# First pair of the up-projection as plain products, with new orders at three stage changes, in a one-core decoder trunk

## The chip, the cores and the metric

One Trainium2 chip, one of its cores. The metric is the device time of one execution of the whole program, in microseconds (us); the kernel before has a median of 1436.61 us over 3 runs (1431.98 to 1438.98).

## The reference, cut to what matters

```python
def reference(x, norm_mix, w_in, ..., w_out, norm_ffn, w_up, conv_w, conv_b, w_down):
    h = rms_norm(x, norm_mix[i])
    proj = h @ w_in[i]
    ...                      # three token mixers: NSA, S5, stick-breaking
    merged = (merge_g[:, :, 0] * (o_a @ w_br_nsa[i])
              + merge_g[:, :, 1] * (o_b @ w_br_s5[i])
              + merge_g[:, :, 2] * (o_c @ w_br_sb[i]))
    x = x + merged @ w_out[i]
    x = x + conv_ffn(rms_norm(x, norm_ffn[i]), w_up[i], conv_w[i], conv_b[i], w_down[i])

def conv_ffn(h, w_up, conv_w, conv_b, w_down):
    u = h @ w_up
    u = causal depthwise convolution of width 3 over the tokens, + conv_b
    gate, val = jnp.split(u, 2, axis=-1)
    return (jax.nn.gelu(gate) * val) @ w_down
```

x is 1024 tokens by 1024 features, float32; w_up is 1024 by 4096, w_down 2048 by 1024.

## The kernel before, in words

Every float32 product is made of three fp32r products (`mm3`, L910 to L914): each operand is split into a high part (an ACT or POOL copy that rounds to fp32r) and a low part (the operand minus its high part), and high by high, high by low and low by high are summed in PSUM. So one 128x128 by 128x512 block costs three MATMUL instructions on PE.

**The token-mixing part** ends with 8 merge panels for the NSA branch (P_NSAMERGE + k, k from 0 to 7, called M+k here) and 8 output panels (P_OUT + k, k from 0 to 7). SP loads each panel into one of two `raw` slots, POOL splits it (`split_panel`, L772 and L775), PE multiplies it. Each merge panel is 60 MATMULs, each output panel 48.

**The sums of down-projection weights.** The up- and the down-projection use a Strassen-Winograd scheme: 7 half-size products in place of 8, on sums of blocks of the weights and of the activations. For the down-projection the four weight sums V are made ahead, beside the last merge panels, in 8 rounds e: SP loads four 128x512 blocks into `vsum` (`load_v`, L599), POOL adds them in place (`sum_v`, L845, four instructions), SP stores them to DRAM (`save_v`, L605). There is one `vsum` buffer, in `arena2`: the load of round e+1 waits for the store of round e. POOL does the sum of round e right after it has split panel M+1+e, so POOL's order is split, sum, split, sum, 8 times, the last after the split of P_OUT.

**The second norm.** When the residual x2 is complete, ACT and DVE normalise it in 8 tiles of 128 tokens (`norm_tiles`, L1540, L1891), PE transposes them (`norm_transposes`, L929) in two halves of tokens T0 and T1, 8 groups of 128 features each. Half T0 is split straight out of PSUM into hTh and hTl (ACT L1551, DVE L1899). Half T1 is handled by the code after that: in this order the kernel before makes the low sums s3, s4, s2 and so on that the Winograd scheme wants (ACT L1828 to L1841, DVE L2418 to L2436, POOL L888, L895, L900), for the four kinds of left operand "n2", "s1", "s4", "s3" of `UP_LEFT`, kept in `hxh`/`hxl` (12 blocks each) and in hTh/hTl.

**The up-projection** has 16 column pairs j (128 gate columns and 128 value columns). A pair is 7 pieces i = 0 to 6 of 12 MATMULs each (`up_product`). `STREAM` lists all pieces in the order of PE; every weight piece n of it is made high by ACT (`weight_high`, L1764) and low by POOL (`weight_low`, L868), with the pair's weight sums on POOL (`weight_sum`, L863) in between. Slots: 5 for raw weights, 5 for the split ones; piece n on ACT waits until PE has used piece n-5. Between pieces ACT copies PSUM banks (`copy_x`, `copy_z`) and DVE adds them (`up_add`, L2445); piece 3 of a pair waits for the copy after piece 1, piece 4 for the one after piece 2. After piece 6, ACT starts the convolution (`conv_first`, L1773) and DVE adds the two other taps (L2453, L2455), ACT applies the GELU and DVE multiplies (L2464, `ffn_pair`).

```python
        STREAM = [(0, 0), (0, 1), (1, 0), (0, 2), (0, 3), (0, 4), (1, 1), (0, 5), (1, 2), (0, 6), (1, 3), (1, 4)]
        for j in range(2, 16):
            STREAM += [(j, 0), (j - 1, 5), (j, 1), (j - 1, 6), (j, 2), (j, 3), (j, 4)]
```

**The down-projection** has 56 pieces ("dn", c) of 12 MATMULs, 7 products m of 8 pieces. Activations are split in 28 halves-pairs f, high by ACT (`dn_high`, L1815), low by DVE (`dn_low`, L2492), with sums of activation blocks before (`dn_sum`, L2478 to L2484) and in place after (L2497, L2502). Product m is added to the output by DVE (`y_out`, L2515), and product m+2 or so, which reuses its PSUM banks, waits for it (`DN_AFTER`). Six of the activation blocks had been spilled to DRAM and are read back (`act_back`, L725).

## Time and profile before

| what | value |
|---|---|
| median of 3 runs | 1436.61 us |
| the profiled execution, its own time | 1430.5 us |
| its span, first to last instruction | 1428.8 us |
| mean granted TensorE clock | 0.978 of 2.4 GHz |
| PE / DVE / POOL / ACT busy | 93% / 55% / 44% / 36% |

The span is cut in 40 slices of 35.7 us in the profile's second part; PE is at 9 tenths or more in most of them, with clear dips in the first slice and around slice 27 (929 to 964 us). The stages at the end are: NSA merge panels from 708 us, output panels from 819 us, the norm from 914 us, the up-projection from 918 us (in steady repetition from 987 us), the down-projection from 1260 us.

### The profile page before, as it was taken

To read this page: it belongs to the slowest core of one execution; us is meant where nothing else is said; L and a number is where in the kernel's file an instruction comes from. 1 tells how busy PE (TensorE), PEld (TensorE's weight loads), DVE (VectorE), ACT (ScalarE), POOL (GpSimd) and SP (SyncE) were. 2 spreads that over 40 slices of the span, in tenths; PEclk is the share of its full clock that TensorE was granted. 3 is DMA by queue.
4 is the path that set the end of the run, shared out by engine and by line. 5 is a ranking of instruction groups with operands and counts; after the bars stand their busy time and mean duration, and the time that the engine had idled before them with its cause. 6 is when DMAs were issued, how large, how long until landed. Compare 5 with 4: busy or idle time off the path is not lost.

```text
span 1428.8 us, 18621 instructions
## 1 busy us (share of the span) xinstructions
PE 1332.2 (93%) x7133; PEld 1052.1 (74%) x7133; DVE 784.8 (55%) x1281; ACT 510.4 (36%) x971; POOL 627.8 (44%) x418
## 2 busy tenths in 40 slices
PE   5999889999999899999899989859999999999998
PEld 4888456799777666666688868637888888877886
DVE  5797576534554766666535211563444444469932
ACT  5422554400111244444311100444454554454431
POOL 4212003234723111101267653578777777756642
PEclk9999999999999999999999999969999999999999
DMA  7430101042111000000145451302222111155433
GB/s 188 47 54 19 45 1 31 16 79 56 38 31 44 19 19 19 1 19 19 49 155 182 166 218 52 133 15 70 79 89 74 55 57 54 53 169 184 131 96 140
DMA packets 142007, 106.01 MB, mean 74 GB/s; under 512 B 41680, under 2 KB 115792, under 8 KB 141904
## 3 DMA queue, kind: packets, MB, share of 16 engines
q1 hardware_dynamic: 141920, 104.83, 25.0%
q8 instruction: 57, 0.93, 0.3%
q14 instruction: 30, 0.25, 0.1%
HBM read 84.76 MB, written 20.05 MB: 73 GB/s over the span
## 4 chain that ended last, share of the span: by engine, by line
PE 74%; DVE 9%; POOL 5%; DMA 4%; ACT 4%; issue 3%; SPq 1%; ACTq 0%; DVEq 0%; POOLq 0%
PE ps L912 20%; PE ps L913 19%; PE ps L914 19%; PE ps L1394 3%; POOL arena L845 3%; PE ps L1427 2%; DMA arena<-in_w_down 2%; PE ps L1411 2%; PE ps L1152 1%; DMA v_down<-arena 1%; PE ps L1169 1%; PE ps L1182 1%; DVE arena L1891 1%; PE ps L929 1%; DVE merged L2139 1%
## 5 line engine op out<-in xcount | busy, mean ns | idle before, releaser
L868 POOL TENSOR_TENSOR wl<-raw,wh 128x512 fp32r<-128x512 f32 x168 | 236.4, 1411 | 158.9 <-ACT wh L1764 158.9
L912 PE MATMUL ps<-hTh,wh 128*128 128x512 f32 x752 | 302.8, 403 | 2.7 <-ACT arena L1630 1.9
L914 PE MATMUL ps<-hTh,wl 128*128 128x512 f32 x752 | 294.1, 391 | 0.0
L913 PE MATMUL ps<-hTl,wh 128*128 128x512 f32 x752 | 294.1, 391 | 0.0
L772 POOL TENSOR_TENSOR wh<-raw,zero 128x1280 fp32r<-128x1280 f32 (+2 forms) x37 | 82.1, 2220 | 478.5 <-PE ps L914 463.1
L1764 ACT ACTIVATE wh<-raw 128x512 fp32r<-128x512 f32 x168 | 105.8, 632 | 305.4 <-PE ps L914 248.8
L912 PE MATMUL ps<-wh,hTh 128*128 128x512 f32 (+2 forms) x496 | 174.0, 351 | 6.7 <-DVE conv L2515 3.4
L914 PE MATMUL ps<-wh,hTl 128*128 128x512 f32 (+2 forms) x496 | 173.9, 351 | 0.0
L913 PE MATMUL ps<-wl,hTh 128*128 128x512 f32 (+2 forms) x496 | 173.6, 350 | 0.0
L775 POOL TENSOR_TENSOR wl<-raw,wh 128x1280 fp32r<-128x1280 f32 (+2 forms) x45 | 128.9, 2865 | 94.6 <-ACT wh L1576 91.7
L912 PEld LDWEIGHTS ps<-hTh,wh 128*128 128x128 f32 x752 | 141.7, 188 | 37.4 <-issue 7.2
L914 PEld LDWEIGHTS ps<-hTh,wl 128*128 128x128 f32 x752 | 141.6, 188 | 31.0
L913 PEld LDWEIGHTS ps<-hTl,wh 128*128 128x128 f32 x752 | 141.7, 188 | 27.6 <-issue 0.5
L912 PEld LDWEIGHTS ps<-wh,hTh 128*128 128x128 f32 x496 | 94.4, 190 | 20.3 <-issue 8.1
L2445 DVE TENSOR_TENSOR ps<-ps,small 128x512 f32<-128x512 f32 x48 | 33.4, 695 | 127.7 <-ACT small L1787 119.5
L913 PEld LDWEIGHTS ps<-wl,hTh 128*128 128x128 f32 x496 | 94.3, 190 | 12.0
L914 PEld LDWEIGHTS ps<-wh,hTl 128*128 128x128 f32 x496 | 94.1, 190 | 12.1
L912 PE MATMUL ps<-hxh,wh 128*128 128x512 f32 x192 | 78.2, 407 | 18.5 <-DVE hxl L2433 10.1
L863 POOL TENSOR_TENSOR raw<-raw 128x512 f32<-128x512 f32 x64 | 82.8, 1306 | 2.5 <-DMA raw<-in_w_up 0.3
L2318 DVE TENSOR_REDUCE small<-ps 128x1 f32<-128x512 f32 (+3 forms) x96 | 49.9, 520 | 54.6 <-PE ps L1397 22.3
L913 PE MATMUL ps<-hxl,wh 128*128 128x512 f32 x192 | 77.3, 403 | 0.0
L914 PE MATMUL ps<-hxh,wl 128*128 128x512 f32 x192 | 77.1, 402 | 0.0
(365 smaller groups left out, 2206.5 us busy)
## 6 DMA issues: line engine op xcount, KB each, us to landing
raw<-in_w_in SPq DMA_DIRECT2D x35, 512.0 KB, 3.9
raw<-in_w_up SPq DMA_DIRECT2D x64, 256.0 KB, 2.8
arena<-in_w_down SPq DMA_DIRECT2D x32, 256.0 KB, 3.4
v_down<-arena SPq DMA_DIRECT2D x32, 256.0 KB, 2.5
raw<-v_down SPq DMA_DIRECT2D x32, 256.0 KB, 2.6
raw<-in_w_down SPq DMA_DIRECT2D x24, 256.0 KB, 2.8
merged<-in_x SPq DMA_DIRECT2D x8, 512.0 KB, 7.3
raw<-in_w_out SPq DMA_DIRECT2D x8, 512.0 KB, 4.6
```

The costliest lines, as they stand in the source:

```text
L772: eng.tensor_tensor(wh[:, p, 0:n], raw[:, p, 0:n], zero1[:, 0:1].broadcast_to((P, n)), ALU.add).then_inc(s_hi[0], 1)
L775: eng.tensor_tensor(wl[:, p, 0:n], raw[:, p, 0:n], wh[:, p, 0:n].bitcast(F32), ALU.subtract).then_inc(s_lo, 1)
L845: eng.tensor_tensor(to, a, b, ALU.add).then_inc(S("v_sum"), 1)
L863: eng.tensor_tensor(to, a, b, ALU.add).then_inc(S("fw_split"), 1)
L868: eng.tensor_tensor(wlf[:, w_slot(n)], raw_piece(n), whf[:, w_slot(n)].bitcast(F32), ALU.subtract).then_inc(S("fw_split"), 1)
L912: mm(out_, ah, bh, start=first, stop=False, skip_group_check=True)
L913: mm(out_, ah, bl, start=False, stop=False, skip_group_check=True)
L914: return mm(out_, al, bh, start=False, stop=last, skip_group_check=True)
L1394: ins = mm(ps[:, bank, 0:w], qT[0:rows, m, h, :], kT[0:rows, kb * P:kb * P + w], start=True, stop=not (edge or diag), skip_group_check=True)
L1764: eng.activation(whf[:, w_slot(n)], raw_piece(n), ACT.Copy).then_inc(S("fw_hi"), 1)
L2318: ins = eng.tensor_reduce(one if single else parts[off // 4], ps[:, 4 + i % 3, 0:nb * P], AX.X, ALU.max, negate=True)
L2445: tt(to, to, x_copy[:, :], ALU.add).then_inc(S("up_add"), 1)
```

## The change

**V sums.** `vsum` becomes two buffers, one in `arena2` and one in `arena3`. Rounds 0 and 1 are loaded together, after all NSA products with V are done. POOL does the sums after the splits of M+1 to M+6, then after those of P_OUT+2 and P_OUT+3. **Pair 0** of the up-projection is no longer in 7 pieces but done plainly: four weight pieces (w11, w21, w12, w22), `plain_half(k, hf)`, 96 MATMULs in place of 84. All raw weights of pair 1 can then be loaded once pieces (0, 0) to (0, 3) are made low. **The sums of half T1** are now made straight from PSUM, after its plain split. **Orders of the down-projection**: dn_low(0) to dn_low(2) one step earlier, dn_high(7) and up one pair earlier, y_out(m) one pair earlier, act_back loaded two pieces earlier.

```diff
-        vsum = [arena2[:, HALF * i:HALF * (i + 1)] for i in range(4)]
+        vsum = [[t[:, HALF * i:HALF * (i + 1)] for i in range(4)] for t in (arena2, arena3)]
...
-        STREAM = [(0, 0), (0, 1), (1, 0), (0, 2), (0, 3), (0, 4), (1, 1), (0, 5), (1, 2), (0, 6), (1, 3), (1, 4)]
+        STREAM = [(0, i) for i in range(4)] + [(1, i) for i in range(5)]
...
+        V_AFTER = {P_NSAMERGE + k: e for e, k in enumerate((1, 2, 3, 4, 5, 6, 10, 11))}
...
             def load_v(e):
-                if e:
-                    eng.wait_ge(S("v_saved"), 64 * e)
+                if e >= 8:
+                    return
+                if e >= 2:
+                    eng.wait_ge(S("v_saved"), 64 * (e - 1))
...
                 if p == P_NSAMERGE + 2:
                     eng.wait_ge(S("pT_ps"), NPC)
-                if P_NSAMERGE + 3 <= p < P_NSAMERGE + 11:
-                    save_v(p - P_NSAMERGE - 3)
-                if P_NSAMERGE + 2 <= p < P_NSAMERGE + 10:
-                    load_v(p - P_NSAMERGE - 2)
+                    eng.wait_ge(S("pv_nsa"), len(PV_OPS))
+                    load_v(0)
+                    load_v(1)
+                if p - 2 in V_AFTER:
+                    save_v(V_AFTER[p - 2])
+                    load_v(V_AFTER[p - 2] + 2)
...
-                if piece == ("dn", 8):
+                if piece == ("dn", 6):
                     used(eng, AT[15, 4])
                     eng.wait_ge(S("act_out"), 96)
-                if j == "dn" and 8 <= name < 14:
+                if j == "dn" and 6 <= name < 12:
...
             for n in range(3):
                 weight_piece(n)
-            eng.wait_ge(S("v_saved"), 512)
             for c in range(KC):
                 eng.wait_ge(S("n2lo"), c + 1)
                 eng.tensor_tensor(hx32[:, c if c < 4 else c + 4, :], hTh[:, c, T0].bitcast(F32),
                                   hTl[:, c, T0].bitcast(F32), ALU.add).then_inc(S("h_pool"), 1)
-            for n in (3, 4):
+                if c == 3:
+                    weight_piece(3)
+            for n in range(4, AT[1, 4]):
                 weight_piece(n)
             for c in range(4):
-                eng.wait_ge(S("n2hi"), 22 + 2 * c)
-                for k in (c, 8 + c):
-                    eng.tensor_tensor(hxl[:, k, :], hx32[:, k, :], hxh[:, k, :].bitcast(F32), ALU.subtract
-                                      ).then_inc(S("h_pool"), 1)
-            weight_piece(5)
-            for c in range(4):
-                eng.wait_ge(S("n2hi"), 29 + c)
-                eng.tensor_tensor(hTl[:, c, T1], low32[:, c, T1], hTh[:, c, T1].bitcast(F32), ALU.subtract
+                eng.wait_ge(S("n2hi"), 25 + c)
+                eng.wait_ge(S("n2lo"), 33 + c)
+                eng.tensor_tensor(hxl[:, c, :], hx32[:, c, :], hxh[:, c, :].bitcast(F32), ALU.subtract
                                   ).then_inc(S("h_pool"), 1)
...
+            def plain_half(k, hf):
+                for kc in range(KC):
+                    n = AT[0, 2 * k + kc // 4]
+                    if hf == 0 and kc % 4 == 0:
+                        eng.wait_ge(S("fw_split"), W_COUNT["low", n])
+                    if k == 0:
+                        eng.wait_ge(S("n2lo"), (9, 11, 13, 15, 17, 18, 19, 20)[kc] if hf else kc + 1)
+                    t = T1 if hf else T0
+                    w = slice(w_slot(n).start + kc % 4 * P, w_slot(n).start + (kc % 4 + 1) * P)
+                    ins = mm3(ps[:, 2 * k + hf, :], whf[:, w], wlf[:, w], hTh[:, kc, t], hTl[:, kc, t],
+                              kc == 0, kc == KC - 1)
+                    if hf and kc % 4 == 3:
+                        ins.then_inc(S("fw_used"), 1)
...
             norm_transposes("n2", 0)
-            up_product(0, 0)
+            plain_half(0, 0)
             norm_transposes("n2", 1, range(4))
-            up_product(0, 1)
+            plain_half(1, 0)
             norm_transposes("n2", 1, range(4, KC))
-            for j, i in STREAM[2:]:
+            plain_half(0, 1)
+            plain_half(1, 1)
+            for j, i in STREAM[4:]:
...
+            for g in range(8, 16):
+                h_high(g)
+                if g < 12:
+                    h_plain(g)
+            weight_high(4)
+            weight_high(5)
...
+            for g in range(8, 12):
+                h_low(g, 2 * g - 6)
+                h_s3(g, 2 * g - 6)
+            for g in range(12, 16):
+                h_low(g, g + 5)
             for c in range(4):
-                stt(hx32[:, 4 + c, :], ps[:, n_bank(12 + c, "n2"), :], gain2[:, 4 + c:5 + c], hx32[:, 4 + c, :],
+                stt(hx32[:, 4 + c, :], ps[:, n_bank(12 + c), :], gain2[:, 4 + c:5 + c], hx32[:, 4 + c, :],
                     ALU.mult, ALU.subtract).then_inc(S("n2lo"), 1)
...
             for n, (j, i) in enumerate(STREAM[:AT["dn", 2]]):
                 if (j, i) in ADD_COUNT:
                     up_add(j, i)
+                if (j, i) == (1, 1):
+                    ffn_pair(0)
                 if j != "dn" and i == 6:
                     ffn_pair(j)
-                if j == 15 and 2 <= i < 5:
-                    dn_low(i - 2)
+                if j == 15 and 1 <= i < 4:
+                    dn_low(i - 1)
             dn_low(3)
             for f in range(4, NPAIR):
-                if f >= 11 and f % 4 == 3:
-                    y_out((f - 11) // 4)
+                if f >= 10 and f % 4 == 2:
+                    y_out((f - 10) // 4)
```

The order of instructions shows the moves. First DVE after the norm's second half of tiles, up to the first add of the up-projection. Of the kernel before:

```order
L2418 SCALAR_TENSOR_TENSOR low<-ps,minus_gain,hx 128x512 x4
L2422 SCALAR_TENSOR_TENSOR hx<-ps,gain,hx 128x512 x4
L2426 SCALAR_TENSOR_TENSOR hx<-hx 128x512
L2430 SCALAR_TENSOR_TENSOR hx<-hx 128x512
L2433 TENSOR_TENSOR hxl<-hx,hxh 128x512
...
L2436 SCALAR_TENSOR_TENSOR hTl<-ps,gain,hTh 128x512 x4
```

(the three rows L2426, L2430, L2433 stand four times). Of the change, from the last of four alternations of L2455 and L2462:

```order
L2462 SCALAR_TENSOR_TENSOR hxh<-ps,minus_gain,hx 128x512
L2455 SCALAR_TENSOR_TENSOR hTl<-ps,gain,hTh 128x512 x4
L2472 SCALAR_TENSOR_TENSOR hx<-ps,gain,hx 128x512 x4
L2475 SCALAR_TENSOR_TENSOR hx<-ps,minus_gain,hxh 128x512 x4
L2479 TENSOR_TENSOR hxl<-hx,hxh 128x512 x4
L2484 SCALAR_TENSOR_TENSOR hx<-hx 128x512 x4
L2488 TENSOR_TENSOR hTl<-hxh,hTh 128x512 x4
L2492 TENSOR_TENSOR hxl<-hx,hxh 128x512 x4
L2501 TENSOR_TENSOR ps<-ps,small 128x512
```

All instructions that read PSUM stand first now, and 16 that read SBUF alone follow, where there were 12; only one up_add stands before the taps of pair 0, where four stood.

POOL around the first output panels, of the kernel before (wh and wl are the split of a panel, arena the V sums):

```order
L845 TENSOR_TENSOR arena<-arena 128x512 x4
L772 TENSOR_TENSOR wh<-raw,zero 128x1024
L775 TENSOR_TENSOR wl<-raw,wh 128x1024
L845 TENSOR_TENSOR arena<-arena 128x512 x4
L772 TENSOR_TENSOR wh<-raw,zero 128x1024
L775 TENSOR_TENSOR wl<-raw,wh 128x1024
```

and of the change:

```order
L782 TENSOR_TENSOR wh<-raw,zero 128x1024
L785 TENSOR_TENSOR wl<-raw,wh 128x1024
L782 TENSOR_TENSOR wh<-raw,zero 128x1024
L785 TENSOR_TENSOR wl<-raw,wh 128x1024
L782 TENSOR_TENSOR wh<-raw,zero 128x1024
L785 TENSOR_TENSOR wl<-raw,wh 128x1024
L855 TENSOR_TENSOR arena<-arena 128x512 x4
```

The last two sums stand behind the splits of P_OUT+2 and P_OUT+3; three output panels are split with no sum between.

DVE in the down-projection, of the kernel before, from the in-place sum of pair f = 10 on:

```order
L2497 TENSOR_TENSOR act_back<-act_back 128x2x512
L2478 TENSOR_TENSOR low<-act 128x2x512
L2492 TENSOR_TENSOR hTl<-low,hTh 128x2x512
L2497 TENSOR_TENSOR act_back<-act_back 128x2x512
L2515 TENSOR_TENSOR conv<-conv,ps 128x512 x4
```

and of the change:

```order
L2553 TENSOR_TENSOR act_back<-act_back 128x2x512
L2571 TENSOR_TENSOR conv<-conv,ps 128x512 x4
L2534 TENSOR_TENSOR low<-act 128x2x512
L2548 TENSOR_TENSOR hTl<-low,hTh 128x2x512
L2553 TENSOR_TENSOR act_back<-act_back 128x2x512
```

The output of product 0 (conv<-conv,ps) stands three instructions earlier.

## Rows read from the trace of the kernel before

**Rows 1.** The page: PE's busy tenths in 40 slices of the span.
```profile
PE   5999889999999899999899989859999999999998
```
**Rows 2.** PE's waits, 850 us to the end: total us, times, longest us.
```profile
PE ps L912 <- DVE hxl L2433: 10.1, 4, 4.0
PE ps L912 <- DVE res L2515: 1.1, 1, 1.1
```
**Rows 3.** PE's timeline at the second output panel: start us, us, [idle before].
```profile
829.99 0.40 PE L914 MATMUL ps<-wh,first_l 128*128 128x512 f32 x1
835.67 0.79 PE L912 MATMUL ps<-wh,first_h 128*128 128x512 f32 x1 [5.29 <-POOL wl L775]
839.59 0.40 PE L912 MATMUL ps<-wh,hTh 128*128 128x512 f32 x1
```
**Rows 4.** The same stretch: busy time of each engine, then PE's granted clock.
```profile
830.00:840.00 10.00, 4.71 (x13) 3.47 (x12) 0.00 (x0) 0.00 (x0) 9.68 (x6) 0.66 0.59 211
```
**Rows 5.** POOL's timeline, last V sums and the split after them.
```profile
808.95 5.39 POOL L845 TENSOR_TENSOR arena<-arena 128x512 f32<-128x512 f32 x4 [5.11 <-DMA arena<-in_w_down]
824.38 6.97 POOL L845 TENSOR_TENSOR arena<-arena 128x512 f32<-128x512 f32 x4 [5.70 <-DMA arena<-in_w_down]
833.28 2.34 POOL L775 TENSOR_TENSOR wl<-raw,wh 128x1024 fp32r<-128x1024 f32 x1
```
**Rows 6.** The chain that ended last, one V round: start us, us, what.
```profile
783.74 2.73 DMA v_down<-arena
...
787.81 5.15 DMA arena<-in_w_down
```
**Rows 7.** PE's timeline from the last output panel to the steady up-projection.
```profile
917.91 0.48 PE L912 MATMUL ps<-hTh,wh 128*128 128x512 f32 x1
928.63 3.04 PE L929 MATMUL ps<-ident,arena 128*128 128x128 f32 x13 [1.19 <-DVE arena L1891]
931.32 0.62 PE L912 MATMUL ps<-hTh,wh 128*128 128x512 f32 x1
934.31 1.91 PE L929 MATMUL ps<-ident,arena 128*128 128x128 f32 x16
987.50 0.39 PE L912 MATMUL ps<-hTh,wh 128*128 128x512 f32 x1
```
**Rows 8.** DVE's timeline, sums of half T1 in the kernel before.
```profile
943.61 1.75 DVE L2433 TENSOR_TENSOR hxl<-hx,hxh 128x512 fp32r<-128x512 f32 x1
953.21 2.71 DVE L2436 SCALAR_TENSOR_TENSOR hTl<-ps,gain,hTh 128x512 fp32r<-128x512 f32 x4
```
**Rows 9.** POOL's timeline in the same stretch.
```profile
941.42 6.74 POOL L895 TENSOR_TENSOR hxl<-hx,hxh 128x512 fp32r<-128x512 f32 x4
949.45 6.22 POOL L895 TENSOR_TENSOR hxl<-hx,hxh 128x512 fp32r<-128x512 f32 x4 [1.29 <-ACT hxh L1837]
955.63 1.26 POOL L868 TENSOR_TENSOR wl<-raw,wh 128x512 fp32r<-128x512 f32 x1
```
**Rows 10.** Busy time of each engine over one steady pair: PE, PEld, DVE, ACT, POOL.
```profile
1206.80:1226.10 19.30, 19.30 (x86) 15.76 (x85) 8.82 (x9) 9.61 (x14) 14.04 (x12) 1.00 0.19 56
```
**Rows 11.** PE's timeline at the down-projection's three waits.
```profile
1260.03 0.47 PE L912 MATMUL ps<-wh,hTh 128*128 128x512 f32 x1 [2.08 <-issue]
...
1308.96 0.39 PE L914 MATMUL ps<-wh,hTl 128*128 128x512 f32 x1
1312.78 0.47 PE L912 MATMUL ps<-wh,hTh 128*128 128x512 f32 x1 [3.43 <-DVE conv L2515]
...
1317.41 0.40 PE L913 MATMUL ps<-wl,hTh 128*128 128x512 f32 x1
```
**Rows 12.** DVE's timeline in the down-projection.
```profile
1307.46 2.31 DVE L2478 TENSOR_TENSOR low<-act 128x1024 f32<-128x1024 f32 x1
1311.96 2.47 DVE L2515 TENSOR_TENSOR conv<-conv,ps 128x512 f32<-128x512 f32 x4
1334.55 2.47 DVE L2515 TENSOR_TENSOR conv<-conv,ps 128x512 f32<-128x512 f32 x4
```

205 lines of the change are left out of this document (114 added, 91 removed).

## The prediction

> **What bounds the kernel now.** I read the page's slices first: PE is busy nine tenths or more nearly everywhere [rows 1], so time is won only where PE stands still or runs at a lower clock, and the dip near 929 to 964 us is the deepest of the late ones. Then PE's waits, its timeline at each of them, and the timelines of the engines that it waits for. PE stands still in the three stages that the change touches. At the second output panel it waits 5.29 us for POOL's split [rows 3]. Between the norm and the steady up-projection the largest waits are for sums made by DVE, 10.1 us in 4 [rows 2], and PE does little there for some 40 us [rows 7]. In the down-projection it waits 2.08 and 3.43 us [rows 11], and 1.1 us for an output add [rows 2]. After each of the long waits the first MATMULs are slow: the granted clock is 0.66 over the ten us around the first of them [rows 4], which is a mixture of the levels 1.2 and 2.4 GHz. A MATMUL at the full level costs 0.23 us of PE (84 in the 19.3 us of a pair [rows 10]).
>
> **Term 1, the V sums.** From 829.99 to 839.59 PE starts ten MATMULs [rows 3]; at 0.23 us they need 2.3 of the 9.6 us, so the stop and the slow clock behind it cost 7.3 us. Its cause is a round of the V loop: the sums start 15.4 us apart (808.95 and 824.38 [rows 5]), made up of the sum (5.4), the store's 2.73 and the load's 5.15 [rows 6], and their issues; a merge panel is 60 MATMULs, 13.9 us. POOL, which must sum before it may split the next panel, falls behind by 1.5 us a round until PE has to wait. With two buffers the loop of one buffer may take two panels, 27.8 us, and needs 15.4. POOL's own work in a panel, about 5.6 us of split (the 1024-wide form's low part is 2.34 [rows 5], the merge form is 1280 wide) and 5.4 of sum, fits in 13.9. The last two sums stand behind the splits of P_OUT+2 and P_OUT+3: 4.2 and 5.4 us in an output panel of 48 MATMULs, 11.1 us. SP now waits longer before its first V load, with the load of panel M+3 behind it on its queue, and issues eight loads at once. That panel is needed only when PE has done one more panel of 13.9 us, so I cost it at nothing; were this cover gone, the first split would be late by the few us of one load. Gain 7.3 us, all on the path; the bounds are 5.3 (the wait alone, if the clock fell all the same) and 7.3.
>
> **Term 2, from the norm to the steady up-projection.** Piece (2, 0) starts at 987.50 [rows 7]. I lay the new order on the same clock. PE begins at 917.91 with plain_half(0, 0), 24 MATMULs, to 923.5. Then it waits as before for the tiles of the second half, until 928.63 [rows 7]: nothing in the change makes them earlier, since ACT's and DVE's orders up to there are the same. The 13 transposes end about 931.4. Now 24 MATMULs, to 937.1; 16 transposes (1.91), to 938.9; 48 MATMULs, to 950.0; and three pieces of pair 1 whose operands are there, to 958.4. So the 12 MATMULs more than before (2.8 us) lie where PE stood still anyhow.
>
> Then PE depends on DVE. DVE's new list starts when ACT has copied the first transposed group of the last four, about 938.4: 12 instructions that read PSUM, 0.68 us each (2.71 for four [rows 8]), to 946.6; then 16 that read two SBUF operands. The price of these is what the forecast hangs on. In the trace such an instruction takes 1.75 us while POOL is at work, and POOL's then take 1.69 in place of 1.26 (6.74 for four [rows 8, 9]); the ones that read PSUM stay at 0.68 beside a busy POOL (DVE at 953.21, POOL from 949.45 [rows 8, 9]). So the two engines take turns, one instruction of each in 1.69 us. POOL has 12 instructions in that stretch (low parts, four hxl, weight sums), so I take 12 at 1.69 and 4 at 0.68: 23.0 us, to 969.6. The ends are 16 at 0.68 (10.9 us) and 16 at 1.69 (27.0 us). Behind them stand the first up_add (0.7) and the two taps of pair 0 (2.6), which piece (2, 0) waits for since it reuses the bank: it starts at 972.9. Pieces (1, 3) and (1, 4) have been done by then: ACT's copy for (1, 3) stands behind its copies that wait for the same DVE list, so PE waits about 6.5 us before (1, 3) and its first MATMULs run at the lower level, but these two pieces end before 972.9. Gain 987.5 - 972.9 = 14.6 us. With 16 at 1.69 it is 10.6; with 16 at 0.68 the DVE list is no longer last, PE waits some 1.5 us for the weight sums of pair 1, does two pieces, and the gain is about 21.9.
>
> The row shows a turn of 1.69 us. The Trainium skill, page "SBUF — State Buffer", section "Who interferes with whom", says that whichever of the two issues first has the shared port pair for the whole instruction and the other fully blocks. By that, a turn would be a POOL instruction of 1.26 and a DVE instruction of 0.68, so 1.94, and the 12 turns would cost 3.0 us more (gain 11.6). The trace shows less, and I go by it.
>
> What the change removes besides: the copies and adds of pair 0 (ACT's three copies of x and one of z, DVE's three adds), the pair's four weight sums on POOL, and POOL's four hxl and four hTl instructions, which DVE now does. Each lay beside the waits counted above and has no price of its own. The loads of pair 1's weights now start when pair 0's are split, long before PE wants them. The changed signs and semaphores cost nothing: no instruction more.
>
> **Term 3, the down-projection.** (a) dn_low(0) is now ahead of the taps of pair 14, so the 2.08 us [rows 11] go: gain 2.1; ends 1 (if dn_low(0) now delays the taps) and 2.1. (b) From 1308.96 to 1317.41 there are 14 MATMUL intervals, 3.2 us at the full level: the stop costs 5.2 us [rows 11]. y_out(0) stood at 1311.96; it now stands three instructions ahead, at 1307.46 [rows 12], and DVE may reach it 1.8 us sooner (my estimate, since act_back comes two pieces, 5.4 us, earlier). This wait goes. But what is late next is y_out(1): 12 instructions stand between the two in both orders, they took 22.6 us from start to start [rows 12], and some ran while PE and POOL stood still; without that pause I take 3 us more. 1305.7 + 25.6 + 0.7 for the first add is 1332.0, and PE comes to product 3 at 1309.2 + 8 x 2.72 = 1331.0. So a wait of 1.0 to 1.5 us stays: gain 4.0, ends 2.0 and 5.2. (c) The last y_out no longer stands behind a dn_low: gain 1.1. Together 7.2.
>
> **Sum.** 7.3 + 14.6 + 7.2 = 29.1 us, against the profiled execution's own 1430.5: 1401.4. The median of the runs shown is 6.1 us above that execution; I put the new median 3.6 above, **1405 us**.
>
> **The rivals.**
> - *DVE and POOL don't meet.* If POOL's order leaves DVE's SBUF list alone, the gain of term 2 is 21.9: 1398. For it: POOL's first two instructions of the list wait for ACT. Against: rows 8 and 9, and POOL's 12 instructions.
> - *They meet more.* 16 turns at 1.69, or the whole-instruction lock of the page above: 3 to 4 us less, 1409.
> - *DVE, not its order, bounds the down-projection.* Every instruction there stands at 2.31 in place of 1.2 us [rows 12], and the wait only moves from y_out(0) to y_out(1): term 3 is 3 us in place of 7.2, 1409.
> - *The change doesn't do what it says to the V loop.* POOL still waits for its first loads, which now start later and two at a time, and the lateness reaches PE at M+2. Worth at most the price of one load and issue, 5 to 6 us of the gain: 1410. Against it is the panel of slack.
> - *Slower.* Pair 0 now ends with no lead: ffn_pair(0) waits on DVE for the GELU, ahead of the adds of pair 1, and each pair hands its lateness on. If a pair of the loop were 2.6 us longer than 19.3, the 14 pairs would eat the 29 us and 7 more: 1444. It decides once an engine other than PE needs over 19.3 us a pair. POOL needs 14.0, DVE 8.8, ACT 9.6 [rows 10]; even 11 POOL instructions at 1.69 are 18.6. So lateness drains, and I give this little.
>
> **How the numbers follow.** Forecast 0.51; DVE and POOL don't meet 0.15; they meet more 0.13; DVE bounds the down-projection 0.12; V loop 0.07; slower 0.02. The first five are all faster by more than 0.5% (7 us, about what a measurement of this kernel can tell from no change); of their 0.98 I leave 0.02 to a sum of misses that ends within it, so faster has 0.96. The range goes from 1393 (the first rival, and a median at the execution's own level) to 1416 (one of the others, with the median 7 above).
>
> **What would show it.** In the changed profile: no wait of PE at the second output panel, sums about a panel apart; PE busy from 928 to 958 less transposes, then one wait of 5 to 8 us before piece (1, 3); DVE's 16 SBUF instructions at 1.7 us for the most; (2, 0) about 22 us before the old time (7.3 and 14.6); no wait for dn_low(0), and one of about 1 us for y_out(1). I am wrong if PE waits for a V sum or a panel load after 708 us, if the steady pair is longer than 19.3 us, or if the wait before (1, 3) is over 12 us.

## The result, and the profile after

The median of the changed kernel is **1400.6 us** over 4 runs (1400.18 to 1402.2), beside 1434.3 us over 4 runs of the kernel before (1431.24 to 1438.98). The ratio is 0.976, with a 95% interval of 0.973 to 0.980: faster by about 34 us. The forecast was 1405.0, the range 1393 to 1416. The profiled execution of the changed kernel took 1400.18 us, 30.3 us less than the profiled one of before (1430.5). Of all executions of the edited kernels below one was slow, of `both` (2200.34 us at a mean granted clock of 0.558), and it is left out of the median given there.

The page of the changed kernel: PE's busy tenths in 40 slices, and the chain that ended last, by engine.

```profile
PE   5999899999999889999999999987999999999998
...
PE 86%; DVE 7%; ACT 3%; issue 2%; POOL 1%; DMA 0%; SPq 0%; ACTq 0%; DVEq 0%; POOLq 0%
```

In [rows 1] slices 24, 26 and 27 stood at 8, 8 and 5; now this part of the span has one dip, slices 27 and 28 at 8 and 7. POOL and the DMAs, which were 5% and 4% of the chain before, are at 1% and 0%. PE's waits from 705 us to the end:

```profile
PE ps L918 <- issue: 7.2, 1, 7.2
PE ps L935 <- DVE arena L1929: 4.0, 3, 1.3
```

The 10.1 us for sums made by DVE and the 1.1 us for an output add [rows 2] are gone, so are the 5.29 at the second output panel [rows 3] and the 2.08 and 3.43 of the down-projection [rows 11]. What is left are the three waits for the norm's tiles and one of 7.2 us before piece (1, 3). "Issue" is the view's word for a wait whose releaser it did not find; the timelines below name it. The kernel before had such a wait too, 7.3 us before a piece of the same stage. It was the longest single wait behind 850 us, and [rows 2] leave it out:

```profile
PE ps L912 <- issue: 9.3, 2, 7.3
```

To see where the time went, take five marks on PE that both kernels have: the first MATMUL of merge panel M, the first transpose of the second norm, piece (2, 0), the first down-projection piece, and the last MATMUL.

| stretch | before, us | after, us | gone | forecast |
|---|---|---|---|---|
| start to M | 708.62 | 707.94 | 0.7 | 0 |
| M to the norm's transposes (term 1) | 205.79 | 197.96 | 7.8 | 7.3 |
| transposes to (2, 0) (term 2) | 73.09 | 60.29 | 12.8 | 14.6 |
| (2, 0) to the first down-projection piece | 272.53 | 270.27 | 2.3 | 2.1 |
| the down-projection | 164.42 | 157.67 | 6.8 | 5.1 |

The last two lines are term 3. The gain from the start to M is in no term, and M's place scatters by more than this. Behind the last MATMUL nothing changed that the marks could tell.

**Term 1.** POOL's timeline, the V sums in the changed kernel:

```profile
741.35 6.39 POOL L855 TENSOR_TENSOR arena<-arena 128x512 f32<-128x512 f32 x4
755.07 6.39 POOL L855 TENSOR_TENSOR arena<-arena 128x512 f32<-128x512 f32 x4
...
833.55 5.38 POOL L855 TENSOR_TENSOR arena<-arena 128x512 f32<-128x512 f32 x4
```

None of these waits for a DMA, where both of [rows 5] did (only the first of the eight sums still does). The first two start 13.72 us apart, a panel of PE, where those of before were 15.4 apart. At the second output panel PE does not stop and the clock stays up: where [rows 4] had 0.66, this window has 1.00 (the granted clock is the third number from the right).

```profile
830.00:840.00 10.00, 10.00 (x45) 8.13 (x44) 0.00 (x0) 0.00 (x0) 8.62 (x6) 1.00 1.00 397
...
950.00:960.00 10.00, 2.84 (x9) 1.96 (x9) 10.00 (x7) 5.16 (x9) 9.87 (x7) 0.66 0.18 52
960.00:970.00 10.00, 10.00 (x38) 8.05 (x37) 8.56 (x8) 4.16 (x6) 7.56 (x6) 0.83 0.18 52
```

**Term 2.** The other two windows hold the one long wait that is left. DVE's timeline (start, us) shows the new list: 12 instructions that read PSUM, 16 that don't, one add, two taps.

```profile
931.20 2.73 DVE L2455 SCALAR_TENSOR_TENSOR hTl<-ps,gain,hTh 128x512 fp32r<-128x512 f32 x4 [3.83 <-ACT hTh L1841]
...
939.11 5.36 DVE L2479 TENSOR_TENSOR hxl<-hx,hxh 128x512 fp32r<-128x512 f32 x4
944.39 4.68 DVE L2484 SCALAR_TENSOR_TENSOR hx<-hx 128x512 f32<-128x512 f32 x4
949.00 6.79 DVE L2488 TENSOR_TENSOR hTl<-hxh,hTh 128x512 fp32r<-128x512 f32 x4
955.71 6.80 DVE L2492 TENSOR_TENSOR hxl<-hx,hxh 128x512 fp32r<-128x512 f32 x4
962.43 0.68 DVE L2501 TENSOR_TENSOR ps<-ps,small 128x512 f32<-128x512 f32 x1
963.03 1.27 DVE L2509 SCALAR_TENSOR_TENSOR conv<-ps,convw,conv 128x1023 f32<-128x1023 f32 x1
964.34 1.28 DVE L2511 SCALAR_TENSOR_TENSOR conv<-ps,convw,conv 128x1022 f32<-128x1022 f32 x1
```

The 12 take 7.9 us (931.20 to 939.11), the 16 take 23.3 (939.11 to 962.43); the forecast had 8.2 and 23.0. ACT's timeline shows why PE waited before (1, 3): four copies to hxh, each behind one of DVE's hTl (L2488), stand ahead of the copy that (1, 3) needs (L1809), and PE starts (1, 3) 0.1 us after that copy.

```profile
955.82 0.63 ACT L1879 ACTIVATE hxh<-hx 128x512 fp32r<-128x512 f32 x1 [1.04 <-DVE hTl L2488]
...
957.39 0.58 ACT L1809 ACTIVATE small<-ps 128x512 f32<-128x512 f32 x1
```

PE's timeline over the same stretch:

```profile
958.07 0.76 PE L918 MATMUL ps<-hxh,wh 128*128 128x512 f32 x1 [7.16 <-issue]
...
963.63 0.39 PE L919 MATMUL ps<-hxl,wh 128*128 128x512 f32 x1
...
966.19 0.40 PE L918 MATMUL ps<-hTh,wh 128*128 128x512 f32 x1
```

(1, 3) and (1, 4) ran at the lower level (1.2 GHz) up to 963.3, took 8.1 us in place of 5.5, and ended 0.6 us after the two taps were done. So (2, 0) starts without a wait, but DVE's list and PE's slow pieces end together there.

**Term 3.** DVE's timeline, the first two y_out (L2571), beside [rows 12]:

```profile
1280.41 2.47 DVE L2571 TENSOR_TENSOR conv<-conv,ps 128x512 f32<-128x512 f32 x4
...
1304.11 2.46 DVE L2571 TENSOR_TENSOR conv<-conv,ps 128x512 f32<-128x512 f32 x4
```

From the first down-projection piece (1236.46) to y_out(0) it is 43.95 us, before it was 51.93 (1260.03 to 1311.96). y_out(1) follows 23.7 us later, and its first add is done 67.6 + 0.7 = 68.3 us after the first piece, where PE comes to product 3 at about 71. No wait is left in the down-projection.

### The profile page after: what moved, and what is told of

Its sections match the earlier page's. It is cut to its first block, busy times and chain, and to the rows that moved or that the text cites. A ratio compares the mean times of both kernels' runs of the same rounds, so it can differ in the third digit from the quotient of the medians.

```text
span 1398.5 us, 18627 instructions
## 1 busy us (share of the span) xinstructions
PE 1326.8 (95%) x7145; PEld 1053.0 (75%) x7145; DVE 803.9 (57%) x1290; ACT 507.1 (36%) x968; POOL 615.0 (44%) x403
## 3 DMA queue, kind: packets, MB, share of 16 engines
q1 hardware_dynamic: 141920, 104.83, 25.6%
## 4 chain that ended last, share of the span: by engine, by line
PE 86%; DVE 7%; ACT 3%; issue 2%; POOL 1%; DMA 0%; SPq 0%; ACTq 0%; DVEq 0%; POOLq 0%
PE ps L918 24%; PE ps L920 23%; PE ps L919 23%; PE ps L1400 3%; PE ps L1433 2%; PE ps L1417 2%; PE ps L1158 1%; PE ps L1175 1%; PE ps L1188 1%; PE ps L935 1%; DVE arena L1929 1%; DVE merged L2177 1%; DVE small L2371 1%; ACT arena L1559 1%; PE ps L1132 1%
## 5 line engine op out<-in xcount | busy, mean ns | idle before, releaser
L918 PE MATMUL ps<-hTh,wh 128*128 128x512 f32 x768 | 309.0, 402 | 2.7 <-ACT arena L1649 1.9
L920 PE MATMUL ps<-hTh,wl 128*128 128x512 f32 x768 | 300.3, 391 | 0.0
L919 PE MATMUL ps<-hTl,wh 128*128 128x512 f32 x768 | 300.0, 391 | 0.0
L1783 ACT ACTIVATE wh<-raw 128x512 fp32r<-128x512 f32 x165 | 102.6, 630 | 246.7 <-PE ps L920 204.9
L918 PEld LDWEIGHTS ps<-hTh,wh 128*128 128x128 f32 x768 | 144.7, 188 | 37.9 <-issue 7.0
L919 PEld LDWEIGHTS ps<-hTl,wh 128*128 128x128 f32 x768 | 144.9, 189 | 28.3 <-issue 0.5
L873 POOL TENSOR_TENSOR raw<-raw 128x512 f32<-128x512 f32 x60 | 78.5, 1321 | 2.2
L918 PE MATMUL ps<-hxh,wh 128*128 128x512 f32 x180 | 72.4, 402 | 7.2 <-issue 7.2
L1649 ACT ACTIVATE arena<-ps 128x512 f32<-128x512 f32 x34 | 20.3, 597 | 157.7 <-PE ps L920 157.7
L1400 PE MATMUL ps<-arena 65*128 65x512 f32 (+7 forms) x192 | 73.9, 468 | 2.6 <-ACT arena L1743 2.6
```

Of the source, the lines that this page charges most:

```text
L873: eng.tensor_tensor(to, a, b, ALU.add).then_inc(S("fw_split"), 1)
L918: mm(out_, ah, bh, start=first, stop=False, skip_group_check=True)
L919: mm(out_, ah, bl, start=False, stop=False, skip_group_check=True)
L920: return mm(out_, al, bh, start=False, stop=last, skip_group_check=True)
L1400: ins = mm(ps[:, bank, 0:w], qT[0:rows, m, h, :], kT[0:rows, kb * P:kb * P + w], start=True, stop=not (edge or diag), skip_group_check=True)
L1783: eng.activation(whf[:, w_slot(n)], raw_piece(n), ACT.Copy).then_inc(S("fw_hi"), 1)
```

## The experiments

Each kernel is an edit of the changed kernel ("after" below). Besides the medians, the stretches between the five marks are compared: they repeat within 0.2 us from one kernel to the next where nothing was edited, except two that depend on where the clock falls (last section). Whole times scatter more, since the start of M alone lay between 707.6 and 714.5 us in kernels whose code up to there is the same. Here are all stretches in us, the last column being from M to the last MATMUL.

| kernel | M to norm | norm to (2, 0) | (2, 0) to down | down | sum |
|---|---|---|---|---|---|
| before | 205.79 | 73.09 | 272.53 | 164.42 | 715.8 |
| after | 197.96 | 60.29 | 270.27 | 157.67 | 686.2 |
| v_undone | 207.62 | 58.51 | 270.40 | 157.68 | 694.2 |
| v_onebuf | 200.40 | 58.77 | 270.37 | 157.66 | 687.2 |
| v_order | 197.97 | 60.21 | 270.28 | 157.69 | 686.2 |
| dn_undone | 197.99 | 60.25 | 272.52 | 167.10 | 697.9 |
| dn_yout_only | 198.60 | 58.81 | 272.60 | 161.83 | 691.8 |
| dn_load | 198.48 | 58.74 | 270.36 | 157.66 | 685.2 |
| port_wait | 198.58 | 55.17 | 270.36 | 157.68 | 681.8 |
| pe_order | 198.57 | 57.89 | 270.27 | 157.66 | 684.4 |
| both | 198.01 | 57.88 | 270.36 | 157.69 | 683.9 |
| copy_early | 197.96 | 59.86 | 270.39 | 157.68 | 685.9 |
| sums_late | 198.68 | 54.55 | 272.79 | 157.69 | 683.7 |
| port_late | 197.97 | 52.58 | 274.35 | 157.70 | 682.6 |

### The V sums: buffer or order

**v_undone** takes back both parts of term 1, the second buffer and the places of the last two sums.

```diff
-        vsum = [[t[:, HALF * i:HALF * (i + 1)] for i in range(4)] for t in (arena2, arena3)]
+        vsum = [[t[:, HALF * i:HALF * (i + 1)] for i in range(4)] for t in (arena2, arena2)]
...
-                if e >= 2:
-                    eng.wait_ge(S("v_saved"), 64 * (e - 1))
+                if e:
+                    eng.wait_ge(S("v_saved"), 64 * e)
...
-                    load_v(1)
...
-                    load_v(V_AFTER[p - 2] + 2)
+                    load_v(V_AFTER[p - 2] + 1)
...
-        V_AFTER = {P_NSAMERGE + k: e for e, k in enumerate((1, 2, 3, 4, 5, 6, 10, 11))}
+        V_AFTER = {P_NSAMERGE + k: e for e, k in enumerate((1, 2, 3, 4, 5, 6, 7, 8))}
```

> The changed kernel, but with one buffer for the V sums and a sum after each of the eight splits M+1 to P_OUT, as before. Theory A (the V loop's 15.4 us a round against 13.9 us of PE a panel is the whole of term 1): the wait of about 5.3 us at the second output panel comes back with the slow clock behind it, and the program is 7.3 us longer than the changed one (5.3 to 7.5). Rival B (something else in the change, such as less DMA traffic beside the panels, gave part of it): clearly less than 5 us.

Measured: 1412.18 us median (ratio to before 0.983, 0.980 to 0.987). The stage from M to the norm grows by 9.7 us, over the upper end of the expected 5.3 to 7.5, and the wait at the second output panel is back. PE's timeline of v_undone, each wait for the split of a panel:

```profile
809.27 0.50 PE L917 MATMUL ps<-hTh,wh 128*128 128x512 f32 x1 [1.02 <-POOL wl L784]
824.11 0.50 PE L917 MATMUL ps<-wh,first_h 128*128 128x512 f32 x1 [0.84 <-POOL wl L784]
840.88 0.80 PE L917 MATMUL ps<-wh,first_h 128*128 128x512 f32 x1 [5.30 <-POOL wl L784]
```

It is 1.8 us more than in before. The first load still stands where the change put it, and POOL's first sum starts 7.0 us after M (718.93), where in before it starts 3.2 after (711.80); that is the likely reason for PE's waits at 809 and 824, which before does not have and which make up the 1.8. It was not run apart. Term 1 itself is what before shows against after: 7.8 us.

**v_onebuf** keeps the new order and takes back only the buffer. **v_order** keeps the two buffers and takes back only the order (the last pair of lines of the diff above).

> The changed kernel with one buffer for the V sums, but with POOL's new order (sums after M+1 to M+6, then after P_OUT+2 and P_OUT+3). Theory A1 (it is the order that helps: six rounds fall behind by 1.5 us each, about 8 us, which the lead of a panel still covers, and the two splits without a sum follow at once): 0 to 1 us longer than the changed kernel. Rival A2 (it is the second buffer that helps, the order alone is not enough): PE waits at M+7 or at the first output panel, 3 to 7 us longer.

> Two V buffers kept, but the last two sums back at their old places in the merge panels: the missing corner of the four combinations of buffer and order. v_undone (neither) cost 9.7 us in the stage from the merge to the norm, v_onebuf (order alone) 2.4. Theory A, the second buffer alone is enough, since each round fits in a panel: 0 to 1 us. Theory B, the two output panels of 48 MATMULs leave POOL no room for split and sum whatever the buffers: 2 to 5 us, with a wait of PE at an output panel.

Measured: v_onebuf 1403.93 us (0.977, 0.973 to 0.981), stage 200.40; v_order 1404.37 us (0.978, 0.975 to 0.981), stage 197.97. POOL's timeline of v_onebuf shows sums that still wait for their loads:

```profile
784.77 5.40 POOL L854 TENSOR_TENSOR arena<-arena 128x512 f32<-128x512 f32 x4 [5.69 <-DMA arena<-in_w_down]
800.18 5.39 POOL L854 TENSOR_TENSOR arena<-arena 128x512 f32<-128x512 f32 x4 [4.71 <-DMA arena<-in_w_down]
```

They are 15.4 us apart as before, but behind the second of them, the sixth sum, the next panels are split with no sum between, and POOL catches up; PE waits only twice, 0.51 and 1.40 us, and its MATMULs behind both are at the full level. v_onebuf's 2.4 us lie between its two expectations (0 to 1, and 3 to 7). In v_order the sums stand 13.7 us apart, as in after, and theory A holds. So of the 9.7 us the order alone gives 7.2, the buffer alone 9.7, and both together no more than the buffer: with two buffers the new places of the last two sums are worth nothing.

### The down-projection

**dn_undone** takes back all of term 3: y_out one step later, dn_low behind the taps, the loads of act_back and of the residual two pieces later, and ACT's dn_high in its old places. **dn_yout_only** is the same with the new place of y_out kept (so without the first four lines of this diff). The lines for the loads are those of dn_load, further down.

```diff
-                if f >= 10 and f % 4 == 2:
-                    y_out((f - 10) // 4)
+                if f >= 11 and f % 4 == 3:
+                    y_out((f - 11) // 4)
...
-                if j == 15 and 1 <= i < 4:
-                    dn_low(i - 1)
+                if j == 15 and 2 <= i < 5:
+                    dn_low(i - 2)
...
-                if j == "dn" and 7 <= c < 12:
-                    dn_high(c - 4)
-                if j == "dn" and c >= 11 and c % 2 and (c + 5) // 2 < NPAIR:
-                    dn_high((c + 5) // 2)
+                if j == "dn" and c in (7, 8, 9, 10, 12):
+                    dn_high({7: 3, 8: 4, 9: 5, 10: 6, 12: 7}[c])
+                if j == "dn" and c >= 13 and c % 2 and (c + 3) // 2 < NPAIR:
+                    dn_high((c + 3) // 2)
...
```

> The changed kernel with all of the down-projection's orders as before (dn_low, dn_high, y_out, act_back). The trace of the changed kernel has no wait there at all, so by theory A the three old waits come back whole: 2.2 us at the first piece, 5.2 us at product 2 with its slow clock, 1.2 us at the last product, 8.6 us longer. By my prediction's sum it would be 7.2 us. Rival B (the start of the up-projection, now earlier, has shifted things so that the old orders would no longer hurt): under 4 us.

> The changed kernel with dn_low, dn_high and act_back's loads as before, so that of the down-projection's new orders only y_out's place stays. Theory A (moving y_out alone takes the wait at product 2; 2.2 us come back at the first piece and about 1 at the last product; y_out(1) is then close to late): 3 to 5 us longer than the changed kernel. Rival B (DVE is late because its inputs come late from DRAM, and y_out's place matters little): 6 us or more.

Measured: dn_undone 1412.34 us (0.984, 0.981 to 0.988), dn_yout_only 1409.62 us (0.982, 0.979 to 0.985). By the last two stretches all of term 3 is worth 11.7 us here (439.6 against 427.9), not 8.6; of that y_out's place is 5.2 and the rest 6.5. The 6.5 stand in the range of dn_yout_only's rival B (6 or more), but its reason, inputs that come late from DRAM, is not what the rows below show for the most. The down-projection is 2.7 us longer in dn_undone than before itself showed. Of these, 1.7 is the clock: PE waits 2.08 us before the first piece in both kernels, and behind it the MATMULs of dn_undone run at 1.2 GHz from 1240.0 to 1243.4, while before's stay at 2.4. The other 0.9 to 1.0 is that the third block of act_back lands later beside PE's pieces (ACT waits 4.32 us for it, in before 3.38), and the wait at y_out(0) is 4.38 us for 3.43. PE's timeline of dn_undone at y_out(0):

```profile
1294.12 0.47 PE L918 MATMUL ps<-wh,hTh 128*128 128x512 f32 x1 [4.38 <-DVE conv L2571]
...
1294.69 0.63 PE L920 MATMUL ps<-wh,hTl 128*128 128x512 f32 x1
```

And PE's timeline of dn_yout_only at y_out(1):

```profile
1315.68 0.47 PE L918 MATMUL ps<-wh,hTh 128*128 128x512 f32 x1 [0.78 <-DVE conv L2571]
```

This is the wait that the prediction had expected in the changed kernel itself. It is there only with the old orders and loads at the start of the stage. DVE's timeline of dn_yout_only, first at the third block of act_back, then at the two y_out:

```profile
1272.13 1.23 DVE L2548 TENSOR_TENSOR hTl<-act_back,hTh 128x1024 fp32r<-128x1024 f32 x1 [2.13 <-ACT hTh L1837]
...
1275.52 2.31 DVE L2548 TENSOR_TENSOR hTl<-act,hTh 128x1024 fp32r<-128x1024 f32 x1
...
1291.16 2.47 DVE L2571 TENSOR_TENSOR conv<-conv,ps 128x512 f32<-128x512 f32 x4
...
1314.86 2.47 DVE L2571 TENSOR_TENSOR conv<-conv,ps 128x512 f32<-128x512 f32 x4
```

After the first down-projection piece (1242.22) y_out(0) comes at 48.9 us and y_out(1) at 72.6; in after at 43.95 and 67.7, so DVE has a lead of 5.0 us there. DVE of after does the same block without that wait for ACT's high part:

```profile
1258.36 6.47 DVE L2548 TENSOR_TENSOR hTl<-act_back,hTh 128x1024 fp32r<-128x1024 f32 x3 [0.25 <-ACT hTh L1837]
```

**dn_load** takes back only the two loads.

```diff
-                if piece == ("dn", 6):
+                if piece == ("dn", 8):
...
-                if j == "dn" and 6 <= name < 12:
...
+                if j == "dn" and 8 <= name < 14:
...
-                if piece == ("dn", 13):
+                if piece == ("dn", 15):
...
-                if j == "dn" and name in (13, 17, 21, 25):
-                    load_res({13: 0, 17: 3, 21: 2, 25: 1}[name])
+                if j == "dn" and name in (15, 19, 23, 27):
+                    load_res({15: 0, 19: 3, 23: 2, 27: 1}[name])
```

> Only the loads of act_back and of the residual are put back two pieces later; the orders of DVE and ACT stay. The prediction gave the earlier loads 1.8 us of lead to y_out(0). Theory A, DVE's order decides when y_out(0) runs, the loads are there anyhow: the down-projection stays within 0.7 us of 157.7. Theory B, the landing decides: DVE's first y_out comes about 5 us later (the two pieces) and PE waits 1 to 3 us at the first or the second of them.

Measured: 1402.14 us (0.977, 0.975 to 0.980), the down-projection 157.66 us, no wait of PE: the loads are worth no time, as theory A has it. They do give DVE a lead. The wait at the third block of act_back is back, and behind it stands the landing. ACT's, DVE's and POOL's timelines of dn_load:

```profile
1263.93 1.07 ACT L1837 ACTIVATE hTh<-act_back 128x1024 fp32r<-128x1024 f32 x1 [3.15 <-DMA act_back<-act_spill]
...
1265.03 1.23 DVE L2548 TENSOR_TENSOR hTl<-act_back,hTh 128x1024 fp32r<-128x1024 f32 x1 [1.99 <-ACT hTh L1837]
...
1268.41 1.21 DVE L2548 TENSOR_TENSOR hTl<-act,hTh 128x1024 fp32r<-128x1024 f32 x1
...
1270.24 3.90 POOL L878 TENSOR_TENSOR wl<-raw,wh 128x512 fp32r<-128x512 f32 x2 [2.83 <-ACT wh L1783]
```

y_out(0) comes 44.9 us after the first piece (1236.93 to 1281.84), so 1.0 of the 5.0 us is from the loads. The other 4.0, between dn_yout_only and dn_load, are from the orders of ACT and DVE, in two parts. 1.7 is the slow clock behind PE's wait for dn_low(0) in dn_yout_only: the taps of pair 15, which follow PE, start 14.5 us after the first piece and not 12.9. 2.2 are two DVE instructions behind the third block, which take 2.31 us each in dn_yout_only, where POOL is at work beside them, and 1.21 in dn_load, where POOL waits 2.83 us for ACT's next high part. How much of the orders is ACT's earlier dn_high and how much DVE's earlier dn_low was not run apart.

### From the norm to the steady up-projection

**port_wait** tests that POOL slows DVE down. In after, POOL makes its second four sums of half T0 while DVE scales the last norm tiles; here it waits for them.

```diff
             for c in range(KC):
+                if c == 4:
+                    eng.wait_ge(S("n2xn"), TB)
                 eng.wait_ge(S("n2lo"), c + 1)
```

> The changed kernel with one wait more on POOL: its sums of half T0 for feature blocks 4 to 7 (four instructions) wait until DVE has written all eight normalised tiles. Theory A (DVE's three late tile instructions take 1.3 to 1.56 us in place of 0.76 only because POOL is at work on SBUF beside them): they fall to about 0.76, the transposes of the second half start 2 to 2.6 us sooner, the whole DVE list behind them too, and the program is 2 to 2.5 us shorter. Rival B (the tile instructions are slow for another reason, such as the store of x2 or the ACT's accumulations): no change, or longer by the delay of POOL's sums.

Measured: 1398.9 us (0.975, 0.972 to 0.978), the stage 5.1 us shorter than in after. DVE's timeline of the four tiles, first and last, in port_wait (all four take 0.75):

```profile
917.82 0.75 DVE L1931 TENSOR_SCALAR arena<-merged,rowss 128x1024 f32<-128x1024 f32 x1
...
920.93 0.75 DVE L1931 TENSOR_SCALAR arena<-merged,rowss 128x1024 f32<-128x1024 f32 x1
```

And in after:

```profile
914.29 0.76 DVE L1929 TENSOR_SCALAR arena<-merged,rowss 128x1024 f32<-128x1024 f32 x1
915.42 1.30 DVE L1929 TENSOR_SCALAR arena<-merged,rowss 128x1024 f32<-128x1024 f32 x1
916.89 1.50 DVE L1929 TENSOR_SCALAR arena<-merged,rowss 128x1024 f32<-128x1024 f32 x1
918.50 1.56 DVE L1929 TENSOR_SCALAR arena<-merged,rowss 128x1024 f32<-128x1024 f32 x1
```

The mechanism holds: DVE's four take 3.00 us and not 5.12. POOL's four sums take 5.03 us alone, and 6.76 in after. The gain is more than the expected 2 to 2.5, because the clock does not fall at the norm at all: behind PE's three waits (0.5 to 0.8 us each, in after 1.3) the 13 transposes take 1.64 us and not 3.04, and the granted clock is 1.00 from 917 to 954 us, where in after it was at the lower level from about 919.1 to 925.6. Against the kernels in which the clock fell elsewhere (58.5 to 58.8 us) the gain is 3.3 to 3.6. The list of DVE itself takes as long as in after, and starts earlier: 20.6 us after the first transposes, not 25.3.

**pe_order** puts plain_half(1, 0), whose operands are there, ahead of the transposes of half T1 that wait for the tiles. **both** joins it with port_wait.

```diff
             plain_half(0, 0)
+            plain_half(1, 0)
             norm_transposes("n2", 1, range(4))
-            plain_half(1, 0)
```

> The changed kernel with PE doing plain_half(1, 0) ahead of the first transposes of the second half. It fills the wait of about 5 us there, so that the clock does not fall, and the last four transposed groups come once their banks are free. Theory A (PE's position sets when DVE's last list starts: 931.2 us in the changed kernel, about 927.5 here): 3 to 4 us shorter. Rival B (ACT and DVE set the start of that list, PE's wait was free): within 0.7 us of the changed kernel.

> Both of the two edits above: POOL's wait and PE's order. Theory A: the gains add in part, since the tiles' end now leads to the transposes only after the 48 MATMULs of half T0 are done (about 920.5 us): 4 to 6 us shorter than the changed kernel. Rival B: no more than the better of the two.

Measured: pe_order 1400.21 us (0.976, 0.973 to 0.979); both 1402.71 us (0.978, 0.974 to 0.981). The stage is 57.89 and 57.88 us, 2.4 under after: for pe_order between its expectations (3 to 4 us, and under 0.7), for both as its rival B has it. PE has less idle time and DVE's list starts at 21.8 us after the first transposes, 3.5 earlier than in after. But it then takes longer. DVE's timeline of both:

```profile
940.47 5.71 DVE L2481 TENSOR_TENSOR hxl<-hx,hxh 128x512 fp32r<-128x512 f32 x4
946.11 5.79 DVE L2486 SCALAR_TENSOR_TENSOR hx<-hx 128x512 f32<-128x512 f32 x4
```

These eight are 1.5 us longer than in after: the list meets one or two more of POOL's instructions. In both the list starts no earlier than in pe_order, 1.2 us later than in port_wait, since the two edits take away the same idle time; so both is worse than port_wait alone. An order that keeps PE busy is of little use where DVE is last.

**copy_early** puts ACT's copy for piece (1, 3) ahead of its four copies to hxh.

```diff
             conv_first(0, 1)
+            copy_x(1, 1)
             for c in range(4):
                 eng.wait_ge(S("n2lo"), 37 + c)
...
-                if j != "dn" and i in (1, 3, 5):
+                if j != "dn" and i in (1, 3, 5) and (j, i) != (1, 1):
                     copy_x(j, i)
```

> The changed kernel with ACT's copy for piece (1, 3) ahead of the four copies that wait for DVE's list. Theory A (DVE's list through the taps of pair 0 ends at 965.6 us and piece (2, 0) at 966.2 waits for it, so freeing piece (1, 3) earlier is worth little): PE's wait moves from before (1, 3) to before (1, 4) and (2, 0), 0 to 1 us shorter. Rival B (ACT's queue is what holds PE, 7.2 us): 4 us or more shorter.

Measured: 1403.44 us (0.977, 0.974 to 0.980), the stage 0.4 us shorter. The wait moves to (1, 4) (5.79 us) and one of 1.48 comes before (2, 0), as theory A has it: ACT's order decides where PE waits, DVE's list how long.

**sums_late** tests the price of DVE's 16 instructions. POOL's weight sums for pieces (1, 5) and (1, 6) go behind the low part of (2, 0) and wait for the end of the list, and ACT's copies for (1, 3) and (1, 4) go ahead of hxh. **port_late** is this with port_wait.

```diff
-                W_STEPS += [("sum", j, 1)] if i == 1 else [("sum", j, 3), ("sum", j, 4)] if i == 4 else []
+                W_STEPS += [("sum", j, 1)] if i == 1 else [("sum", j, 3), ("sum", j, 4)] if i == 4 and j > 1 else []
+                W_STEPS += [("sum", 1, 3), ("sum", 1, 4)] if (j, i) == (2, 0) else []
...
+                if (j, i) == (2, 0):
+                    eng.wait_ge(S("n2lo"), 44)
+                    weight_sum(1, 3)
+                    weight_sum(1, 4)
...
+            copy_x(1, 1)
+            copy_z(1)
             for c in range(4):
                 eng.wait_ge(S("n2lo"), 37 + c)
...
```

> After, with POOL's two weight sums (1, 3) and (1, 4) moved behind the low part of piece (2, 0) and held until DVE's list of 44 is done, and ACT's copies for pieces (1, 3) and (1, 4) moved ahead of its four copies to hxh. So POOL has some 8 instructions beside DVE's 16 SBUF-SBUF ones and not 12 to 13. Theory A, the two engines take turns: four to five DVE instructions fall from 1.70 to about 0.68 us, the 16 take 18 to 19.5 us and not 23.3, and the stage from the norm's transposes to piece (2, 0) is 3.5 to 4.7 us shorter than the 60.3 of after. Theory B, DVE is slow there for a reason that is not POOL: the 16 stay at 23 us and the stage within 0.5 us. Theory C, the sums come too late for piece (1, 5), which is wanted 2.7 us after (2, 0) starts: the stage is shorter, but PE then waits 1 to 4 us before (1, 5), and the gain is given back behind the mark.

> The POOL wait of port_wait and the later weight sums of sums_late together, as a candidate for the fastest. Theory A, the first moves the start of DVE's list and the second shortens the list, so they add: a further 3.5 to 4.7 us below port_wait, the stage 51 to 52 us and the whole 1394 to 1396 us. Theory B, once the list is shorter another wait decides (POOL's four differences for piece (1, 3), or the weight sums for (1, 5)): no more than 2 us below port_wait.

Measured: sums_late 1398.5 us (0.975, 0.973 to 0.978), port_late 1397.75 us (0.975, 0.972 to 0.978). DVE's timeline of sums_late:

```profile
938.38 5.34 DVE L2486 TENSOR_TENSOR hxl<-hx,hxh 128x512 fp32r<-128x512 f32 x4
943.65 4.69 DVE L2491 SCALAR_TENSOR_TENSOR hx<-hx 128x512 f32<-128x512 f32 x4
948.26 5.79 DVE L2495 TENSOR_TENSOR hTl<-hxh,hTh 128x512 fp32r<-128x512 f32 x4
953.98 3.58 DVE L2499 TENSOR_TENSOR hxl<-hx,hxh 128x512 fp32r<-128x512 f32 x4
```

The last instruction of L2495, in a narrower window:

```profile
953.37 0.68 DVE L2495 TENSOR_TENSOR hTl<-hxh,hTh 128x512 fp32r<-128x512 f32 x1
```

The 16 now take 19.1 us (the add behind them starts at 957.48) and not 23.3. POOL starts 8 instructions beside them, where it started 12 (and a 13th in the last 0.5 us). Four fewer take 4.2 us off the list, 1.06 us each. One by one: an instruction of the list alone takes 0.60 us from start to start (953.37 to 953.98; its own 0.68 overlaps the next), one in a turn 1.67 to 1.71. After has 3 alone, 12 in turns and the first at 1.29, beside a POOL instruction that had started 0.5 us before: 1.8 + 20.2 + 1.3 = 23.3. Sums_late has 7, 8 and 1: 4.2 + 13.6 + 1.3 = 19.1. So a meeting costs DVE about 1.1 us in both, and the number of meetings is what the list's length hangs on.

Piece (2, 0) starts 5.7 us earlier (4.2 of the list, 1.1 of an earlier start of it), but 2.5 of it are given back at once. PE's timeline of sums_late, from (2, 0) on:

```profile
960.82 0.47 PE L923 MATMUL ps<-hTh,wh 128*128 128x512 f32 x1 [2.24 <-DVE conv L2518]
...
961.93 0.63 PE L924 MATMUL ps<-hTl,wh 128*128 128x512 f32 x1
...
971.38 0.47 PE L923 MATMUL ps<-hTh,wh 128*128 128x512 f32 x1 [0.52 <-ACT small L1814]
```

After the wait before (2, 0) the clock falls inside (2, 0), and the next copy comes late as well. Theory A holds for the list, and the stage gains more than its 3.5 to 4.7. Of theory C the give-back holds but not its wait for the sums before (1, 5). Net it is 2.5 us from M to the end. In port_late 4.1 us are given back, 2.1 of them as a wait for ACT's copy, which stands behind high parts that wait for POOL's late sums and for a DMA. The sum of its stretches (682.6) is no better than port_wait's (681.8): expectation B. By the medians port_wait, sums_late and port_late can't be told apart from each other, and none of them with certainty from after; by the marks **port_wait is the best**, 4.4 us under after in the sum and 3.4 under dn_load, whose code in these stages is after's.

## Why the prediction was right, and where it was off

**Term 1 (7.3 forecast, 7.8 measured)** was right in cause and size: the round of 15.4 us against a panel of 13.9, and POOL's lateness. In five of the edited kernels whose code is after's up to the norm, this stage took 198.5 to 198.7 us, which makes it 7.1 to 7.3. The eight V loads at once cost nothing. What it did not see: with two buffers the new places of the last two sums are not needed (v_order), and with them one buffer would have been nearly enough (v_onebuf).

**Term 2 (14.6 forecast; 12.8 in the profiled run).** The step on which the prediction hung, 12 instructions of 16 at a turn of 1.69 us, gave 23.0 us for 23.3 measured, and sums_late shows that it is the number of POOL's instructions that sets it. The other reading, by the Trainium skill, page "SBUF — State Buffer", section "Who interferes with whom" (the shared port pair is an exclusive lock, held for the whole instruction), made a turn 1.94 us and the list 26.0; the turns measured are 1.67 to 1.71, so the trace does not agree with it in full. Two terms of the sum were off. DVE's list began 25.3 us after the first transposes, not 24.0: the tile waits and the 13 transposes were as the prediction had them from [rows 7], but of the 24 MATMULs behind them, which it had laid at the full level, seven ran at the lower one. And pieces (1, 3) and (1, 4), said to "end before 972.9" with room, took 8.1 us at the lower level and ended last by 0.6. In four edited kernels with the same code in this stage only one or two of those 24 MATMULs were slow, the list began 23.9 to 24.2 us after the first transposes, and the stage took 58.5 to 58.8 us; the forecast was 58.5 (914.41 to 972.9).

**Term 3 (7.2 forecast, 9.0 measured).** Part (a) was right: 2.1 forecast, 2.3 measured. In part (b) the step that failed is "a wait of 1.0 to 1.5 us stays". It was worked out from a lead of 1.8 us that the earlier loads of act_back were to give, and from 25.6 us between the first two y_out. Both were mis-sized. y_out(0) came 3.5 us earlier after the first piece than by its place alone (43.95 against 47.4, which is 1307.46 - 1260.03), and y_out(1) followed in 23.7, so no wait is left. Of the 3.5 us the loads gave 1.0 (dn_load). 2.2 are two DVE instructions that no longer run beside POOL, by ACT's and DVE's orders at the stage's start, which the prediction had costed at nothing beyond (a). With loads and orders undone the forecast wait is there, 0.8 us. So the mechanism was right, and the lead was too small and put down to one edit of two.

**The rivals.** DVE and POOL do meet, at the forecast price, which settles the first two. DVE does not bound the down-projection. That rival also misread its row: [rows 12] show one instruction at 2.31 us, and of the 12 between the first two y_out of before six took 2.3 and six 1.21. The V loop did what it says. No pair hands lateness on: PE has no wait at all from (2, 0) to the end. Of the signs named, those for the second output panel, for the 7.2 us before (1, 3), for the 16 instructions and for dn_low(0) were found; (2, 0) came 21.3 us earlier, for 22, with 0.7 of it from ahead of M; the one for y_out(1) was not.

**The sum** was 29.1 us and the profiled executions differ by 30.3, of which 0.7 lies ahead of M. That it fits so well is luck in part: term 2 was 1.8 us too high and term 3 1.8 too low. The forecast is 4.4 us above the median for another reason: it put the new median 3.6 us over the execution's own time, as before's was 6.1 over its. The changed kernel's median is 0.4 over its own.

## What to carry to other kernels

Where two engines slow each other down on SBUF, price a list of instructions by counting the other engine's instructions that will run beside it, with the turn read from the trace before; moving four of those away gave 4.2 us of the list. Then ask what stands behind the list: 2.5 to 4.1 us of such a gain went to the next late copy and to the clock. And when several edits of one stage go together, undo them one at a time: here the second buffer made the new order idle, and the earlier loads gave DVE a lead of 1.0 us that nothing needed.
